# The order of the matmuls inside one MLP product of a hybrid encoder layer

## The reference, cut to what matters

```python
mix = jnp.concatenate([_rmsnorm(y_hy, hy_out_norm_w), _rmsnorm(y_mla, mla_out_norm_w)], axis=-1)
x = x + mix @ w_out
h = _rmsnorm(x, mlp_norm_w) @ w_mlp1        # (tokens, 1024) @ (1024, 4096)
x = x + jnp.square(jax.nn.relu(h)) @ w_mlp2 # (tokens, 4096) @ (4096, 1024)
gate = jax.nn.sigmoid(x @ w_ple_gate)
x = x + gate * _rmsnorm(p_l @ w_ple_proj, ple_norm_w)
```

## Time and profile before

| | us |
|---|---|
| median of 3 runs (lowest, highest) | 1772.93 (1771.71, 1774.05) |
| profiled execution, first to last instruction | 1772.0 |
| TensorE busy | 1726.4 (97%), 10539 matmuls, 10539 weight loads |
| VectorE busy | 1304.7 (74%) |
| ScalarE busy | 730.8 (41%) |
| GpSimd busy | 394.2 (22%) |
| matmuls of line 3292 (the MLP products) | 5376, first start 813.7, last 1621.0 |
| chain that ended last | TensorE 81%, VectorE 9%, transfers 3%, ScalarE 3% |
| mean granted TensorE clock | 0.995 of full speed |

### The profile page before, as it was taken

The page is one execution under the profiler, slowest core; times in us unless marked ns, Lnnn a source line. Parts: engine busy times, 40 slices in busy tenths (PEclk is TensorE's granted clock), DMA queues, the critical chain, the costliest instruction groups (busy, mean ns, idle before and its releaser), DMA issues.

```text
span 1772.0 us, 26325 instructions
## 1 busy us (share of the span) xinstructions
PE 1726.4 (97%) x10539; PEld 1577.8 (89%) x10539; DVE 1304.7 (74%) x1622; ACT 730.8 (41%) x1150; POOL 394.2 (22%) x252
## 2 busy tenths in 40 slices
PE   7999999998999999999999999999899999999999
PEld 5776878877999988888999999999899999998887
DVE  6894676878998987679755555557989797974634
ACT  6122321167787786146333333334333333334411
POOL 0000000002222220002122221223748283730000
PEclk9999999999999999999999999999999999999999
DMA  9324254151100023433332222329240505101121
GB/s 362 127 72 131 71 201 139 42 184 44 58 22 22 16 84 99 144 122 125 108 110 88 101 100 88 107 77 354 74 156 25 190 1 178 37 31 48 36 95 60
DMA packets 58929, 182.98 MB, mean 103 GB/s; under 512 B 6901, under 2 KB 7669, under 8 KB 58296
## 3 DMA queue, kind: packets, MB, share of 16 engines
q1 hardware_dynamic: 58808, 181.30, 29.0%
HBM read 138.25 MB, written 43.02 MB: 102 GB/s over the span
## 4 chain that ended last, share of the span: by engine, by line
PE 81%; DVE 9%; DMA 3%; ACT 3%; issue 2%; SPq 1%; POOL 0%; DVEq 0%; ACTq 0%
PE ps L3292 40%; PE ps L2768 22%; PE ps L3152 3%; PE ps L3180 3%; PE ps L3164 2%; PE ps L2828 2%; PE ps L2855 2%; PE ps L2867 2%; DVE ptl L2364 1%; DVE gmax L2317 1%; DMA K<-decay 1%; PE ps L3061 1%; DMA wst<-wb 1%; DMA wst<-wm 1%; PE ps L3073 1%
## 5 line engine op out<-in xcount | busy, mean ns | idle before, releaser
L3292 PE MATMUL ps<-rV,ringh 128*128 128x320 f32 x1248 | 235.6, 311 | 6.4 <-DVE X L2602 4.4
L3292 PE MATMUL ps<-rU,ringh 128*128 128x320 f32 x1088 | 204.1, 309 | 3.2 <-issue 2.8
L3292 PEld LDWEIGHTS ps<-rV,ringh 128*128 128x128 f32 x1248 | 197.3, 189 | 7.5 <-DVE X L2602 4.6
L2768 PE MATMUL ps<-XL,wh 128*128 128x512 f32 x708 | 178.0, 360 | 0.0
L3292 PEld LDWEIGHTS ps<-rU,ringh 128*128 128x128 f32 x1088 | 170.6, 188 | 4.2 <-issue 4.1
L2542 DVE TENSOR_TENSOR fH<-ps,fH 128x640 f32<-128x640 f32 x112 | 90.7, 822 | 112.0 <-PE ps L3292 111.8
L2768 PE MATMUL ps<-XH,wh 128*128 128x512 f32 (+1 forms) x612 | 163.1, 375 | 6.9 <-DVE wl L1678 3.4
L2768 PE MATMUL ps<-XH,wl 128*128 128x512 f32 (+1 forms) x588 | 147.6, 360 | 0.0
L3292 PE MATMUL ps<-rV,ringl 128*128 128x320 f32 x624 | 142.8, 310 | 0.0
L3292 PE MATMUL ps<-rH,ringh 128*128 128x320 f32 x736 | 137.8, 309 | 1.3 <-DVE rH L2490 1.3
L2768 PEld LDWEIGHTS ps<-XL,wh 128*128 128x128 f32 x708 | 118.5, 190 | 21.1
(11 more groups left out here) (415 smaller groups left out, 3854.3 us busy)
## 6 DMA issues: line engine op xcount, KB each, us to landing
hd<-fH SPq DMA_DIRECT2D x64, 320.0 KB, 2.3
wst<-wb SPq DMA_DIRECT2D x34, 512.0 KB, 4.0
wst<-wm SPq DMA_DIRECT2D x30, 512.0 KB, 4.1
fU<-hd SPq DMA_DIRECT2D x32, 320.0 KB, 4.3
fH<-hd SPq DMA_DIRECT2D x24, 320.0 KB, 5.2
wraw<-wm SPq DMA_DIRECT2D x14, 512.0 KB, 3.7
w2b<-wm SPq DMA_DIRECT2D x12, 512.0 KB, 6.3
xraw<-xT SPq DMA_DIRECT2D x8, 640.0 KB, 9.7
```

Source lines behind the costliest of these rows:

```text
L2768: ins = mm(acc(jslot)[:, o:o + n], sub(a[slot], s), b[:, o:o + n], start=(first and k == 0 and a is wh and b is xh), stop=(last and k == l ...
L3292: ins = mm(out[:, c, :], a[:, w], two(b(xs[kk]))[:, c, :], start=fresh and kk == 0 and a is h and b is hi_of, stop=kk == 3 and a is l, ski ...
```

## The change

Inside `product` the loop over the two banks (c) moves from innermost to outermost: first all four k-steps with their three terms for c = 0, then the same for c = 1. The operand waits stand in the first pass only, since the second reads the same tiles. Flags (`start`, `stop`) belong to the same matmuls as before, and `mm_done` is signalled by the last one.

```diff
+import itertools
...
                 out = slot(i)
-                for kk in range(4):
-                    if waits:
+                for c, kk in itertools.product(range(2), range(4)):
+                    if waits and c == 0:
                         pe.wait_ge(*waits[kk])
                     w = slice(kk * P, (kk + 1) * P)
                     for a, b in ((h, hi_of), (h, lo_of), (l, hi_of)):
-                        for c in range(2):
-                            ins = mm(out[:, c, :], a[:, w], two(b(xs[kk]))[:, c, :],
-                                     start=fresh and kk == 0 and a is h and b is hi_of, stop=kk == 3 and a is l, skip_group_check=not fresh)
+                        ins = mm(out[:, c, :], a[:, w], two(b(xs[kk]))[:, c, :],
+                                 start=fresh and kk == 0 and a is h and b is hi_of, stop=kk == 3 and a is l, skip_group_check=not fresh)
                 ins.then_inc(mm_done, 1)
```

## The result

| | before | after |
|---|---|---|
| median of 18 runs, us | 1771.77 (1769.55 to 1774.57) | 1773.76 (1772.23 to 1779.77) |
| ratio, 95% interval | | 1.0014 (1.0007 to 1.0020) |
| profiled execution, first to last instruction, us | 1772.0 | 1770.7 |
| first MLP matmul to the start of product 7, us | 32.3 | 34.35 |
| product 7 to product 112, us | 371.5 | 371.9 |

The change costs 0.14%, 1.2 to 3.5 us: real, but under the 0.2% that the forecast called "the same". The forecast of 1773.6 us stands beside 1773.76. That closeness is luck: the median of before moved from 1772.93 (3 runs) to 1771.77 (18 runs), so the measured step is +2.5 us by the ratio where the forecast had +0.7.

What follows compares the result with a forecast made beforehand. TensorE, busy for 97% of the span, was taken to bound the kernel through matmul count times spacing. Adding +0.7 us from closer waits and 0 from bank changes to the median of 1772.93 gave 1773.6 us; range 1766 to 1778.

Steps and rivals of the forecast that it cites:

- The pace: All 5376 MLP matmuls: 4928 fewer bank changes alter nothing at 146.7 ns each; zero, within 0.6 us.
- The faster rival: All MLP products: each bank change costs 3.7 ns, so 18 us are won, 1755 us; chance 0.13.
- a same-bank row at 228 ns: Line 3061, 512 columns: if same-bank accumulation costs 1.3 ns per MLP matmul, 7 us lost, 1781 us; chance 0.06.
- The second half's waits: Second half of the MLP: no operand comes late; the narrowest group is still 2.2 us early, so no cost.
- the pauses near 1241 and 1253 us: TensorE idle at the second half's entrance, 1.88 and 4.39 us: keeps its lengths, both 0.7 us later.
- Product 0 and product 5: MLP entrance: late operands add 1.32 us behind product 0 and end product 5 at 839.6, not 838.7; VectorE's lateness absorbs both.
- 0.6 us left at product 3: MLP entrance: product 0's 1.32 us delay shrinks to this after product 3's 0.62 us idle, gone at product 5.
- a lower end of 1766: Bottom of the range for the whole kernel's time, set at a third of the faster rival's price.
- Product 6: MLP entrance: 15 matmuls instead of 6 follow the operand awaited until 844.45; product 7 starts 0.75 us later, +0.7 us.
- the clock rival: MLP entrance: late operands unabsorbed (3.5 us) and a clock fall (2.1 us), together 5.6 us, 1778.5 us; chance 0.05.
- The sum: Whole kernel: +0.7 us from closer operand waits, 0 from bank changes; 1773.6 us, called the same.

Runs made afterwards that it cites:

- the six other kernels with the old `linear`: Follow-up variants of the MLP order, with the order in `linear` left as in the kernel before; ratios 1.0002 to 1.0008 where timed, single runs 1776.22 and 1778.83 us.
- the experiment with product 0 alone: Kernel before, with the new loop order in MLP product 0 only; one run, 1776.22 us.
- The timed halves of the change: Kernel before, with the new order only from product 7 on (ratio 1.0004), and only in products 0 to 6 (ratio 1.0003).

## Why the prediction was right, point by point

- The pace: right. 146.7 ns before and after, and free changes between two banks are shown at 512 columns as well. The forecast took 0 and allowed 0.6 us; the first half shows 0.1 to 0.2 us.
- The faster rival (3.7 ns a change, from the triples) is refuted; so is the argument that a same-bank row at 228 ns would cost 7 us. The reason given against the former, that the triple mixes widths, may be its cause; the third bank isn't excluded.
- The second half's waits: right, none binds; the stretch from product 121 on is 362.4 us in both. I had said that the pauses near 1241 and 1253 us would keep their lengths. They didn't: 0.25 and 5.45 us in place of 1.88 and 4.39, together 0.6 us less. No experiment changed only that; from product 112 to 120 the six other kernels with the old `linear` took 34.3 to 35.3 us, the changed one 34.25 and the one before 35.35, so it scatters by about the 1.1 us by which the changed kernel is ahead there. (The table's 1.5 us, to product 121, has some 0.4 of half clock in product 120 besides.)
- Product 0 and product 5: right in the end. The delay is absorbed, and the experiment with product 0 alone shows it even with 2.9 us. It lasts longer than forecast, though: with the half clock behind product 0's pause, product 5 starts 22.00 us after the first MLP matmul (before: 21.38) and has lost its own pause, and only product 6's late operand takes up the rest. (The working has 0.6 us left at product 3 where 1.32 less 0.62 is 0.7, and a lower end of 1766 where a third of 18 us gives 1767; neither matters.)
- Product 6: the mechanism was right and its size too small. The step that failed is the sentence in the clock rival that "product 6's pauses get shorter or stay". In pass c = 0 there are 3 matmuls between waits instead of 6, so a pause grows by 3 x 0.147 = 0.44 us: the last two from 0.68 to 1.11. With that the clock fell within product 6, and the 15 matmuls that must follow the last operand ran in large part at 267 ns. Term of the sum: +0.7 forecast, +2.1 measured at the entrance, of which 0.75 is the longer queue of matmuls and 1.3 the clock. I had this cost as a rival, but placed its fall behind product 0's pause, where it is absorbed, and gave it 0.05 together with a lack of absorption that has nothing to do with it.
- The sum: +0.7 us, within what counts here as the same, but below the interval of +1.2 to +3.5 us. Entrance +2.1 and the first half's +0.3 make 2.4 us, which is in it, if the 1.5 us that the profile after gains from product 112 to 121 are scatter; with them the two profiled MLPs differ by only 1.0 us. That they are scatter is likely, since over all eleven profiles this stretch takes 39.5 to 41.4 us, with the new order there as without it. The timed halves of the change (1.0004 and 1.0003, each within 0.1%) don't confirm the split, and the second lies a little low for it; it rests on the timelines and the clock.

## What to carry to other kernels

An order of loops inside a product is also an order of waits: count the matmuls that stand behind the last operand to arrive, and those between one late operand and the next. Splitting a tiled matmul by output bank makes the pauses between early waits longer and the tail behind the last one longer as well; both lengthenings showed, and neither came from the price of a bank. Where TensorE is saturated, look for rounds that mix widths over three banks, which cost 12 ns each here, before looking at how often the bank changes.

## What the runs showed of the hardware that I had not expected

- With a weight load for each, matmuls of one width start every 120 ns at 256 columns, 146.7 at 320 and 227 at 512, which is 13.3 to 13.8 ns more than the columns take at 2.4 GHz. At 320 and 512 columns this is so whether they stay in their PSUM bank or alternate between two. It doesn't hold for narrow ones: those of 128 columns at line 3164 start 109 ns apart.
- 512, 512 and 256 columns in turn over three banks take 585 ns instead of 574, so such a round costs 11 to 12 ns.
- Within product 6 the clock fell to 1.2 GHz with no pause longer than 1.11 us (three of them, 0.61 to 1.11 us, with 3 matmuls between them), while pauses of 1.31, 0.62, 1.22 us and three of 0.7 us with 6 matmuls between them, all in one entrance, left it at 2.4. The half clock that followed differed between executions: 846.41 - 842.28 = 4.13 us for the same 15 matmuls, against 3.63.
- Thirty-four matmuls whose result nobody reads, put into the pauses of products 0 and 6, won 1.3 us at the entrance.
